# Splitting weight units on GpSimd in four rounds, high half then low half, instead of one high pass and four low pieces

## What is computed

```
for i in range(2):
    m = forgetting_attention(x, ...) if i == 0 else rglru_block(x, ...)
    x = layer_norm(ALPHA * x + m, ln1_g[i], ln1_b[i])
    val, gate = split(causal_dwconv(x @ f_w_up[i]))
    ff = (gelu(gate) * val) @ f_w_down[i]
    x = layer_norm(ALPHA * x + ff, ln2_g[i], ln2_b[i])
    x = x + sigmoid(x @ ple_gate_w[i] + ple_gate_b[i]) * (p[i] @ ple_w[i])
```

## Time and profile before

| | |
|---|---|
| runs | 1378.39, 1373.12, 1373.19 us |
| median | 1373.19 us |
| the profiled execution | 1378.74 us |
| its span, first to last instruction | 1377.0 us |
| busy share PE / PEld / DVE / ACT / POOL | 96% / 75% / 44% / 32% / 66% |
| mean granted TensorE clock | 0.979 |
| `w_lo` (L356) on POOL | 848 instructions, 643.3 us, mean 789 ns |
| `w_hi` (L352) on POOL | 212 instructions, 223.0 us, mean 1052 ns |
| matmuls at L370, L371, L372 on `x` | 896 each, mean 399, 390, 390 ns |

### The profile page before, as it was taken

One profiled execution on the slowest core, in us unless ns is written; L12 is line 12 of the kernel. 1 busy time (PEld: TensorE's weight loads), 2 busy tenths in 40 slices (PEclk: granted clock), 3 DMA queues, 4 the chain that ended last, 5 costly groups with the idle time before them and its releaser, 6 DMA issues.

```text
span 1377.0 us, 18552 instructions
## 1 busy us (share of the span) xinstructions
PE 1319.0 (96%) x5780; PEld 1033.3 (75%) x5780; DVE 601.7 (44%) x878; ACT 437.4 (32%) x703; POOL 914.1 (66%) x1289
## 2 busy tenths in 40 slices
PE   6999999988999999999999699998999999999998
PEld 3666666666888888888878577776888888888876
DVE  6533444275444444413253357175544444313263
ACT  1434343313334333300043257114433433201042
POOL 6434443374798777687876555483987887678854
PEclk9999999996999999999999899998999999999999
DMA  4111111111233232233223222211332332333321
GB/s 177 49 61 46 61 61 46 61 62 61 77 107 107 91 98 84 82 101 98 87 106 122 67 78 70 77 62 61 107 107 91 98 100 74 99 97 86 119 77 61
DMA packets 34024, 116.33 MB, mean 84 GB/s; under 512 B 3728, under 2 KB 5008, under 8 KB 33984
## 3 DMA queue, kind: packets, MB, share of 16 engines
q1 hardware_dynamic: 33008, 113.26, 25.6%
q10 hardware_dynamic: 976, 2.55, 0.5%
HBM read 113.63 MB, written 2.16 MB: 84 GB/s over the span
## 4 chain that ended last, share of the span: by engine, by line
PE 60%; issue 19%; POOL 10%; POOLq 7%; DVE 3%; DVEq 1%; DMA 1%; ACT 0%; SPq 0%; ACTq 0%
PE bank L370 17%; PE bank L372 17%; PE bank L371 17%; POOL w_lo L356 9%; POOLq L353 4%; POOLq L351 2%; PE bank L587 2%; PE bank L590 2%; PE bank L588 2%; PE bank L394 1%; DMA stage<-w_square 1%; DVEq L802 1%; DVE part_total L801 1%; DVE x L790 0%; DVE dist L759 0%
## 5 line engine op out<-in xcount | busy, mean ns | idle before, releaser
L356 POOL TENSOR_TENSOR w_lo<-stage,w_hi 128x256 fp32r<-128x256 f32 (+1 forms) x848 | 643.3, 789 | 31.2 <-issue 0.9
L370 PE MATMUL bank<-x_hi,w_hi 128*128 128x512 f32 x896 | 357.9, 399 | 3.2 <-POOL w_lo L356 1.6
L371 PE MATMUL bank<-x_lo,w_hi 128*128 128x512 f32 x896 | 349.2, 390 | 0.0
L372 PE MATMUL bank<-x_hi,w_lo 128*128 128x512 f32 x896 | 349.1, 390 | 0.0
L350 POOL TENSOR_TENSOR waiter<-waiter 128x1 f32<-128x1 f32 x212 | 46.6, 220 | 382.0 <-PE bank L372 264.3
L352 POOL TENSOR_SCALAR w_hi<-stage 128x1024 fp32r<-128x1024 f32 (+1 forms) x212 | 223.0, 1052 | 33.7 <-issue 33.7
L370 PEld LDWEIGHTS bank<-x_hi,w_hi 128*128 128x128 f32 x896 | 168.5, 188 | 48.0 <-issue 15.9
L372 PEld LDWEIGHTS bank<-x_hi,w_lo 128*128 128x128 f32 x896 | 168.3, 188 | 36.0
L371 PEld LDWEIGHTS bank<-x_lo,w_hi 128*128 128x128 f32 x896 | 168.6, 188 | 31.8
L949 DVE SCALAR_TENSOR_TENSOR tmp<-bank,cols,tmp 128x511 f32<-128x511 f32 x88 | 66.0, 750 | 197.3 <-ACT tmp L1208 186.3
L370 PE MATMUL bank<-h_hi,w_hi 128*128 128x512 f32 x352 | 139.7, 397 | 0.0
(11 more groups left out here) (188 smaller groups left out, 1795.4 us busy)
## 6 DMA issues: line engine op xcount, KB each, us to landing
stage<-w_square SPq DMA_DIRECT2D x164, 512.0 KB, 3.3
stage<-w_down SPq DMA_DIRECT2D x32, 448.0 KB, 3.3
stage<-w_down SPq DMA_DIRECT2D x16, 512.0 KB, 3.5
outT<-x SPq DMA_DIRECT2D x8, 256.0 KB, 2.0
x<-xT SPq DMA_DIRECT2D x2, 512.0 KB, 5.1
x<-xT ACTq DMA_DIRECT2D x2, 512.0 KB, 8.4
p_in<-pT ACTq DMA_DIRECT2D x2, 512.0 KB, 3.4
w_ai<-w_lru SPq DMA_DIRECT2D x1, 1024.0 KB, 6.1
```

The lines of the kernel that those rows point to most:

```text
L356: low = pool.tensor_tensor(w_lo[:, s, to], stage[:, s, to], w_hi[:, s, to].bitcast(F32), ALU.subtract)
L370: pe.matmul(out, w_hi[:, s, c:c + P], m_hi, start=first, stop=False)
L371: pe.matmul(out, w_hi[:, s, c:c + P], m_lo, start=False, stop=False)
L372: return pe.matmul(out, w_lo[:, s, c:c + P], m_hi, start=False, stop=last)
```

## The change

The single `w_hi` pass over the unit and its drain go into the loop over the pieces. Each of the four rounds now makes `w_hi` of a quarter of the columns, drains, and makes `w_lo` of the same quarter. The semaphore is still incremented once, by the last `w_lo`.

```diff
                         pool.tensor_tensor(waiter[:], waiter[:], waiter[:], ALU.mult)
                         pool.drain()
-                        pool.tensor_scalar(w_hi[:, s, 0:w], stage[:, s, 0:w], 1.0, 0.0, ALU.mult, ALU.add)
-                        pool.drain()
                         for c in range(0, w, w // PIECES):
                             to = slice(c, c + w // PIECES)
+                            pool.tensor_scalar(w_hi[:, s, to], stage[:, s, to], 1.0, 0.0, ALU.mult, ALU.add)
+                            pool.drain()
                             low = pool.tensor_tensor(w_lo[:, s, to], stage[:, s, to], w_hi[:, s, to].bitcast(F32),
                                                      ALU.subtract)
                         low.then_inc(unit_split, 1)
```

## The result

The changed kernel takes 1431.7 us (median of 4 runs, 1430.24 to 1434.33) against 1375.79 for the kernel before on the same chip: 1.040 times as long, 95% interval 1.036 to 1.045. The forecast was 1426 us, slower. Its profiled execution took 1432.01 us with a span of 1429.6.

What follows compares the result with a forecast made beforehand. TensorE was taken as the bound, with POOL close behind stage by stage; 1.0 + 3.1 + 20.5 + 4.1 + 20.0 + 4 = +52.7 us, from the median 1373.19 to 1426 us, range 1396 to 1456.

Steps and rivals of the forecast that it cites:

- Bound by stage, not by share: Whole kernel: POOL's margin is 0.75 us per `up` unit against TensorE, not the third of the span its share suggests.
- 1.05 us per unit: POOL's unit: 0.60 us for four quarter `w_hi` plus 0.45 for three more drains, from 4.37 to 5.42 us.
- The first rival: POOL's units: addition stays below the margin at 0.45 to 0.53 us; about +4, 1377 us; chance 0.12.
- The chains: First `up` units to third `gate` unit, 69 units per layer: POOL falls behind TensorE, +20.5 and +20.0 us.
- The rule of the loss: Layer 0, `up0` to `gate0`: loss is 69 x addition - 51.9 us, beginning at 0.75 us per unit.
- TensorE's stop: Start of each `gate` stage: TensorE's L587 stands about 5 us waiting for POOL.
- The clock: Behind the wait at each `gate` start: TensorE's granted clock drops, 2 us each, +4 in all.
- DVE beside `up`: `up` stages: DVE's two-input instructions disturb POOL by 0.3 us per unit, 4.67 against 4.37.
- rival 2: `up` units: POOL meets every DVE two-input instruction in full, 0.69 us per unit; +28, 1454 us; chance 0.15.
- Start: `qkv`: unit 0 comes later, and with it the forget-gate chain that L447 waits for, +1.0 us.
- my third rival: Norm blocks: shorter POOL instructions let DVE in sooner, 2 to 3 us per block; about -10, 1363 us; chance 0.03.
- `out`: `out0` and `out1`: L403 waits on a unit three additions later, +3.1 each; `out1` another +1.0, so +4.1.

Runs made afterwards that it cites:

- The copies alone: Kernel before with four quarter `w_hi` in a row, one drain, then four `w_lo` as before: 1371.39 us, 0.998 of before.
- the drains alone: Kernel before with one `w_hi` per unit but a drain between the four `w_lo`: 1374.16 us, 1.0005 of before.
- the run with the rounds in the chain phases alone: Four rounds only in up, down, ple and gate of both layers, one `w_hi` elsewhere as in the kernel before: 1430.08 us, 1.039 of before.
- the runs with less added: Kernel before with quarter copies and low pieces grouped, one drain per group: two groups of two, 1380.52 us; groups of two, one and one, 1409.37 us.
- the three kernels above: The kernel before, 1375.79 us; the changed kernel, 1431.7 us; the kernel before with `PIECES = 2`, 1389.74 us.
- the control without DVE's pair: Kernel before without DVE's two instructions with two SBUF inputs per pair of `up` units: 1379.23 us, 1.0006 of before.
- the two kernels with `PIECES = 2`: `PIECES` 4 to 2 in the changed kernel (two rounds): 1392.53 us, 1.013; in the kernel before (one `w_hi`, two `w_lo`): 1389.74 us, 1.010.

## Why the prediction was right, point by point

- **Bound by stage, not by share: right.** The copies alone and the drains alone show the margin; the run with the rounds in the chain phases alone shows the place.
- **1.05 us per unit: right** (5.42 against 4.37). The first rival needed 0.53 or less; the fixed part of a short `w_hi` is 0.20 us (0.41 at 256 columns) and all but 0.03 us of it shows behind a `w_lo`. It does hide in part behind another `w_hi` (1.51 us for four), which the prediction did not need. The gap behind a drain stayed at 0.15 us with the shorter instruction ahead of it. The tens of cycles for which the prediction named the Trainium skill (GPSIMD Engine Reference, "Instruction dispatch") are there the price of one indirect call within the dispatch, not of the whole; the 0.20 us are all of the fixed part, so the page does not speak against them.
- **The chains: right in mechanism, undersized.** I had 20.5 and 20.0 us, and 2 each for the clock. From POOL's waiter of the first freed slot to unit 104 it measured 392.1 us against my 387.3: `up0` 230.8 for 228.9, `down0` 131.7 for 132.4, the last five 29.6 for 28.0, and the 2 us of overlap that I took off were not there to take. The rule of the loss, 69 x addition less a constant, needs about 47 in place of my 51.9 to give this, and would begin at 0.68 us, not at 0.75; by the runs with less added it begins between 0.56 and 0.65, and its slope is near 69 but not constant. TensorE's stop was 4.40 us, for my 5. The clock cost 2.3 us each time, where I took 2 from the 1.5 of the earlier trace rows.
- **DVE beside `up`: between forecast and rival 2.** POOL's units in the steady part of `up0` run 5.38, 6.25, 5.45 and 5.96 us in turn, 5.76 on average, where the undisturbed pace is 5.38: 0.38 us each, for my 0.30 and the rival's 0.69 (its sign was a unit over 5.9). The Trainium skill's exclusive lock (SBUF — State Buffer, "Who interferes with whom") agrees in kind with the units that run free once DVE's pair is gone, and with L736's growth in the three kernels above; the full 0.69 us for every unit did not come about.
- **Start: wrong in sign**, +1.0 forecast, -2.5 measured. Unit 0 was ready at 16.63 instead of 16.08, 0.55 us late and not 1.0: POOL spent 6.74 us on it instead of 5.70, but its load had landed 0.5 us earlier in this execution. The forget-gate chain does hang on it: DVE's first step (L836) starts at 18.79 instead of 18.24. The step that failed is that I let this delay go through to L447 unchanged. Behind L836 the chain is small DVE instructions, and POOL's long copies and its `w_lo` pieces in a row had been holding them up; by the end of L843 (26.13 instead of 28.64) the chain is 2.5 us early. Seven dependent instructions at L728, before and then after:

```profile
22.18 4.43 DVE L728 SCALAR_TENSOR_TENSOR fg<-fg 128x64 f32<-128x64 f32 x7
```

```profile
22.22 2.60 DVE L728 SCALAR_TENSOR_TENSOR fg<-fg 128x64 f32<-128x64 f32 x7
```

  One of the seven, in the kernel before, takes 1.06 us beside a copy of POOL that starts 0.05 us ahead of it; four take 0.61 to 0.63 beside `w_lo` pieces; free ones take 0.23. The runs bear the cause out: L447 comes at 26.0 with the rounds in `qkv` alone, at 26.7 with the copies alone and at 27.8 with the drains alone. This is the mechanism of my third rival, in a place where I had not looked for it. I had read TensorE's 3.44 us wait at L447 and not asked what DVE itself had waited for.
- **`out`: somewhat too dear, and hidden by the clock.** From the first L587 of `out` to L403 the kernel before takes 33.9 and 50.3 us and the changed one 36.4 and 53.5: 2.5 lost in `out0` (3.1 forecast) and 3.2 in `out1` (4.1 forecast, its first 1.0 seen in L587's wait, 4.12 for 3.08). The table's 2.0 for `out1` has 1.2 us in it that the stages ahead of `out1` gained. That the block behind it gained 5.5 us is mostly the clock, which fell behind L403 in the profiled execution of before (0.50 from 317 to 332) and only in part in that of after (0.86 from 311 to 326.6).
- **The total: partly luck.** 52.7 us forecast, 52.6 between the two spans, 55.9 between the medians. Some 12 us too little in the chains and their clock (56.9 measured, 44.5 forecast) stand against a start and two `out` stages that I had put 12.6 us too dear (-4.4 for everything outside the chains, 8.2 forecast), among them the 5.5 us of the block behind L403. Against before's runs with the clock up (1371.6) the change costs 60 us.

## What to carry to other kernels

An engine busy for 66% of the span can be within some 0.6 us per unit of being the bound in the stage that matters: compare time per unit, stage by stage, before adding to it, and count the disturbed unit, not the undisturbed one. In this kernel an addition under the margin was free and one over it was paid nearly in full, times the number of units until the next place where the other engine waits for something else. On GpSimd two costs pull apart here: many short instructions cost 0.20 us each and 0.15 us per drain, long ones went with slower VectorE instructions (L728, L736). Where GpSimd had slack, in `qkv`, the short ones gained some 2 us; in `out`, where it had none, they cost 3.4 and 5.0.

## What the runs showed of the hardware

**The clock makes levels.** Runs of the kernel before don't scatter evenly: 23 runs beside the last experiments lie at 1371.5 to 1374.2 (6 runs, mean granted clock 0.983 to 0.986), 1377.8 to 1380.3 (15 runs, 0.977 to 0.979) and 1383.6 to 1384.1 (2 runs, 0.974 to 0.975). The traces point to what the steps are: in the block from L403 to `up`, TensorE has mostly one-column and 128-column matmuls with waits between, and in some traces the clock falls to 0.50 there and in others not; the block then takes 21.2 to 23.1 us instead of 15.8 to 17.3. There is one trace of each kernel, so that the same kernel falling in one execution and not in the next is argued from its times and mean clocks, and not seen in two traces. The length of L403's wait does not settle it: behind 1.58 us the clock fell at `out0` in before and stayed up in the control without DVE's pair, behind 2.02 us at `out1` it was the other way round. With the wait at 0.6 us the block took 15.8 to 16.5 us in every trace that shows this, and with 2.1 us or more, in the two kernels with `PIECES = 2`, it was slow every time in their traces. What decides in between stays open. It also means that a difference of 6 us between two single executions of this kernel, and now and then of 12, is not yet an effect of a change.
